# Retention pairs in a two-layer encoder trunk: three block sums per product set written to PSUM and turned or scaled from there, and a new order for the token sums and decay matrices around them

## What is computed

```python
a = rms_norm(h, norm_g[0, 0])
proj = a @ w_in                                  # (1024, 1024) x (1024, 3328)
q, k, v, g, mq = jnp.split(proj, [768, 1536, 2304, 3072], axis=-1)
qh, kh = rotary(q, pos), rotary(k, pos) * 128 ** -0.5
y = forward(qh, kh, vh, decay[0]) + flip(forward(flip(qh), flip(kh), flip(vh), decay[1]))
# forward, in chunks of 128: scores with decay, plus a state that is scanned over chunks
y = silu(g) * group_norm(y)
m = memory_attention(mq, mem_k, mem_v)           # softmax over 256 keys, scale 1/8
h = h + rms_norm(concatenate([y, m]) @ w_out, norm_g[0, 1])
```

## Time and profile before

| | us |
|---|---|
| median of 3 runs | 2235.84 (2235.43 to 2237.63) |
| profiled execution | 2234.97 |
| its span, first to last instruction | 2233.2 |
| TensorE busy | 2192.5 |
| VectorE busy | 1329.0 |
| GpSimd busy | 1199.2 |
| ScalarE busy | 923.5 |
| mean granted TensorE clock | 0.997 of full speed |

### The profile page before, as it was taken

One profiled execution on the slowest core, in us unless ns is written; L12 is line 12 of the kernel. 1 busy time (PEld: TensorE's weight loads), 2 busy tenths in 40 slices (PEclk: granted clock), 3 DMA queues, 4 the chain that ended last, 5 costly groups with the idle time before them and its releaser, 6 DMA issues.

```text
span 2233.2 us, 31950 instructions
## 1 busy us (share of the span) xinstructions
PE 2192.5 (98%) x11542; PEld 1799.5 (81%) x11542; DVE 1329.0 (60%) x2159; ACT 923.5 (41%) x1851; POOL 1199.2 (54%) x953
## 2 busy tenths in 40 slices
PE   9899999999999999999999999999999999999998
PEld 8678777788888888888889877778878888888887
DVE  6867777847644444577773245555575444447767
ACT  6532222456232332344563345465732333234444
POOL 1256666568988888400324243325799888870001
PEclk9999999999999999999999999999999999999999
DMA  8001111543343323563354523344433433338334
GB/s 330 29 29 48 48 48 48 187 181 104 129 146 122 113 95 109 207 230 91 99 189 116 149 68 91 62 140 154 168 108 121 158 99 108 99 118 323 98 96 164
DMA packets 130970, 280.37 MB, mean 126 GB/s; under 512 B 31983, under 2 KB 46590, under 8 KB 128766
## 3 DMA queue, kind: packets, MB, share of 16 engines
q1 hardware_dynamic: 130814, 278.33, 38.4%
HBM read 207.76 MB, written 70.54 MB: 125 GB/s over the span
## 4 chain that ended last, share of the span: by engine, by line
PE 84%; DVE 6%; POOL 3%; issue 2%; ACT 1%; DMA 0%; DVEq 0%; POOLq 0%; ACTq 0%
PE PS L2692 26%; PE PS L2694 25%; PE PS L2693 25%; PE PS L2967 2%; POOL OPS L1101 2%; PE PS L3233 2%; PE PS L3215 1%; PE PS L3133 1%; DVE rtmp L2540 1%; DVE rtmp L2541 1%; PE PS L3000 1%; PE PS L2954 1%; DVE ST L2471 1%; DVE qT L2542 1%; POOL TW L1125 1%
## 5 line engine op out<-in xcount | busy, mean ns | idle before, releaser
L2692 PE MATMUL PS<-AOP,OPS 128*128 128x512 f32 x1216 | 474.3, 390 | 1.1 <-POOL OPS L1101 0.6
L2694 PE MATMUL PS<-AOP,OPS 128*128 128x512 f32 x1216 | 473.2, 389 | 0.0
L2693 PE MATMUL PS<-AOP,OPS 128*128 128x512 f32 x1216 | 473.1, 389 | 0.0
L1101 POOL TENSOR_TENSOR OPS<-TW,OPS 128x512 fp32r<-128x512 f32 x174 | 263.2, 1526 | 78.6 <-ACT OPS L1464 77.4
L1035 POOL TENSOR_TENSOR wlo<-stage,whi 128x512 fp32r<-128x512 f32 (+1 forms) x120 | 153.7, 1304 | 218.5 <-ACT whi L1357 218.3
L2692 PEld LDWEIGHTS PS<-AOP,OPS 128*128 128x128 f32 x1216 | 228.3, 188 | 51.5 <-POOL OPS L1101 2.4
L2694 PEld LDWEIGHTS PS<-AOP,OPS 128*128 128x128 f32 x1216 | 228.3, 188 | 47.4
L2693 PEld LDWEIGHTS PS<-AOP,OPS 128*128 128x128 f32 x1216 | 228.3, 188 | 47.0
L1464 ACT ACTIVATE OPS<-TW 128x512 fp32r<-128x512 f32 x176 | 106.6, 628 | 343.7 <-POOL TW L1125 321.4
L2692 PE MATMUL PS<-OPS 128*128 128x512 f32 x584 | 227.7, 390 | 0.3
L2694 PE MATMUL PS<-OPS 128*128 128x512 f32 x584 | 227.2, 389 | 0.0
(11 more groups left out here) (339 smaller groups left out, 4755.4 us busy)
## 6 DMA issues: line engine op xcount, KB each, us to landing
stage<-in_w SPq DMA_DIRECT2D x100, 512.0 KB, 3.8
hidden_scratch<-HT SPq DMA_DIRECT2D x154, 256.0 KB, 2.2
SRAW<-hidden_scratch SPq DMA_DIRECT2D x154, 256.0 KB, 2.7
stage<-in_wpack SPq DMA_DIRECT2D x76, 512.0 KB, 3.8
BW<-in_w SPq DMA_DIRECT2D x16, 1024.0 KB, 8.4
h_scratch<-Hb SPq DMA_DIRECT2D x24, 512.0 KB, 3.8
Hb<-h_scratch SPq DMA_DIRECT2D x24, 512.0 KB, 5.9
cat_scratch<-OC SPq DMA_DIRECT2D x14, 512.0 KB, 3.0
```

The costliest lines, as they stand in the source:

```text
L1101: pool.tensor_tensor(place[:, 1, :], w1_operand(l, j, p), place[:, 0, :].bitcast(F32), ALU.subtract)\
L2692: pe.matmul(dst, stat[0], mov[0], start=start, stop=False, skip_group_check=onto)
L2693: pe.matmul(dst, stat[0], mov[1], start=False, stop=False, skip_group_check=onto)
L2694: return pe.matmul(dst, stat[1], mov[0], start=False, stop=stop, skip_group_check=onto)
```

## The change

1. The sums "22", "21" and "12" are written to PSUM: "22" into bank 6, "21" and "12" over their own bank. The rotations and scalings read them there; `turn_pairs` works in the bank and its last operation writes SBUF. Its first operation has no wait behind it any more. A bank is free for its next product only when the rotation or scaling is done (`bank_out`), where it was free after the sum.
2. VectorE's order per head: `query_second` directly behind "21", ahead of "12" and `group_norm`; `key_first` behind `value_first`, ahead of "u3".
3. The first token sum (s_one) is made before memory attention; the further sums move to steps 1 to 4, the remainder to 11 to 14. The decay matrices move to steps 10 to 15 (ScalarE) and 11 to 16 (VectorE).
4. At the first head: ScalarE's `block_hi(0)` comes before the gate and `block_hi(1)` behind it, `token_his_late(0)` behind the values; GpSimd's `block_lo(0)` comes first; `first_sum_lo` goes behind "u2"; two of the four `token_lo_late` go from GpSimd to VectorE, ahead of the scan.

```diff
-            for item in (("u2", a), ("u3", a), ("22", a), ("11", a), ("21", a), ("12", a), ("u2", b), ("query", h), ("11", b),
-                         ("u3", b), ("key", h), ("22", b), ("21", b), ("value", h), ("12", b), ("gate", h)):
+            for item in (("u2", a), ("u3", a), ("22", a), ("11", a), ("22 out", a), ("21", a), ("query", h), ("12", a),
+                         ("u2", b), ("11", b), ("key", h), ("u3", b), ("22", b), ("21", b), ("value", h), ("22 out", b),
+                         ("12", b), ("gate", h)):
...
+        def ret_sum_at(r, which):
+
+            if which in ("u2", "u3"):
+                return ret_block(r, "12" if which == "u2" else "22")
+            return ret_bank({"22": "6", "21": "4", "12": "3"}[which])
+
+        def bank_out(p, r):
+
+            even = r % 2 == 0
+            h = 1 + r // 2
+            return summed(*{"1": ("11", r), "6": ("22 out", r), "7": ("query", h) if even else ("value", h),
+                            "5": ("key", h) if even else ("gate", h)}[p])
...
@@ GpSimd
+                if r == 0:
+                    block_lo(0)
                 weight_sum(r, "5")
                 weight_sum(r, "6")
-                block_lo(7 * r)
+                if r:
+                    block_lo(7 * r)
...
                 if h == 1:
-                    for k in range(4):
+                    for k in range(2, 4):
                         token_lo_late(k)
...
@@ ScalarE
-                if 4 <= t < 4 + RH:
-                    h = t - 4
+                if 10 <= t < 10 + RH:
+                    h = t - 10
...
                     if u == 3:
+                        block_hi(0)
                         act.wait_ge(*EV[n])
                         gate(0)
-                        block_hi(0)
-                if t == steps(RUN_A0) - 1:
-                    act.wait_ge(*USED[U_RETH + 3])
-                    token_his_late(0)
+                        block_hi(1)
...
                     if h == 1:
-                        block_hi(1)
+                        token_his_late(0)
                         block_hi(2)
                         token_his_late(1)
...
@@ VectorE, before memory attention
+            for k in range(4):
+                g1, g2 = gT[:, GAIN[1], k:k + 1], gT[:, GAIN[1], 4 + k:5 + k]
+                link(dve.tensor_scalar(xraw[:, 1, 4 + k, :], xraw[:, 1, 4 + k, :], g2, None, ALU.mult))
+                dve.scalar_tensor_tensor(out=xraw[:, 1, 4 + k, :], in0=xraw[:, 1, k, :], scalar=g1,
+                                         in1=xraw[:, 1, 4 + k, :], op0=ALU.mult, op1=ALU.add).then_inc(s_one, 1)
...
-                if 5 <= t < 5 + RH:
+                if 11 <= t < 11 + RH:
...
@@ VectorE, sums and rotations
-                dve.tensor_tensor(ret_block(r, dst), ret_bank(bank), ret_block(r, with_), ALU.add).then_inc(c_sum, 1)
+                dve.tensor_tensor(ret_sum_at(r, what), ret_bank(need), ret_sum_at(r, with_), ALU.add).then_inc(c_sum, 1)
...
-            def turn_pairs(dst, src, cols):
-
-                link(dve.tensor_tensor(rtmp[0:64, :], src[64:128, :], ropeS[64:128, cols], ALU.mult))
-                link(dve.tensor_tensor(rtmp[64:128, :], src[0:64, :], ropeS[0:64, cols], ALU.mult))
-                link(dve.tensor_tensor(dst, src, ropeC[:, cols], ALU.mult))
-                return dve.tensor_tensor(dst, dst, rtmp[:, :], ALU.add)
+            def turn_pairs(dst, bank, cols):
+
+                dve.tensor_tensor(rtmp[0:64, :], bank[64:128, :], ropeS[64:128, cols], ALU.mult)
+                link(dve.tensor_tensor(rtmp[64:128, :], bank[0:64, :], ropeS[0:64, cols], ALU.mult))
+                link(dve.tensor_tensor(bank, bank, ropeC[:, cols], ALU.mult))
+                return dve.tensor_tensor(dst, bank, rtmp[:, :], ALU.add)
...
             def key_first(r):
 
                 dve.wait_ge(*summed("12", r))
-                dve.wait_ge(*summed("query", r // 2 + 1))
-                turn_pairs(ret_block(r, "12"), ret_block(r, "12"), T0).then_inc(c_sum, 1)
+                turn_pairs(ret_block(r, "12"), ret_sum_at(r, "12"), T0).then_inc(c_sum, 1)
...
@@ VectorE, order of a head
                     product_sum(r, "u2")
+                    if h == 1:
+                        first_sum_lo()
                     block_lo(r)
+                    if h == 1:
+                        for k in range(2):
+                            token_lo_late(k)
                     scan(h, lambda c: product_sum(r, "u3") if c == 3 else None)
                     product_sum(r, "22")
                     query_first(r)
                     key_second(r)
                     product_sum(r, "21")
+                    query_second(r)
                     product_sum(r, "12")
                     group_norm(h)
                     product_sum(r + 1, "u2")
-                    query_second(r)
                     block_lo(r + 1)
                     value_first(r + 1)
+                    key_first(r)
                     product_sum(r + 1, "u3")
-                    key_first(r)
                     product_sum(r + 1, "22")
...
@@ TensorE
                 elif r:
-                    pe.wait_ge(*summed({"1": "11", "6": "u2", "7": "21", "5": "12"}[p], r - 1))
+                    pe.wait_ge(*bank_out(p, r - 1))
```

More of the change, by code:

```diff
@@ L279, in trunk_program @@
         s_one, s_diff, s_two, s_hi, s_lo = sem("s_one"), sem("s_diff"), sem("s_two"), sem("s_hi"), sem("s_lo")
-        s_hi_late, s_lo_one, s_lo_four = sem("s_hi_late"), sem("s_lo_one"), sem("s_lo_four")
+        s_hi_late, s_lo_one, s_lo_four, s_lo_pool = (sem(n) for n in ("s_hi_late", "s_lo_one", "s_lo_four", "s_lo_pool"))
         q_sum, q_hi, q_lo, q_lo_dve, q_used = (sem(n) for n in ("q_sum", "q_hi", "q_lo", "q_lo_dve", "q_used"))
@@ L2504, in token_sums @@
                                              in1=xraw[:, 0, k, :], op0=ALU.mult, op1=ALU.add).then_inc(s_two, 1)
-                if 6 <= t < 10:
-                    k = t - 6
+                if 11 <= t < 15:
+                    k = t - 11
                     dve.wait_ge(s_hi, 2 * k + 1)
@@ L2509, in token_sums, with token_lo_late @@
                                              in1=sum_hi[:, 0, k, :].bitcast(F32), op0=ALU.mult, op1=ALU.subtract).then_inc(s_lo_one, 1)
+            def token_lo_late(k):
+                dve.wait_ge(s_hi_late, 5 + k)
+                dve.tensor_tensor(sum_lo[:, 0, 4 + k, :], xraw[:, 0, 4 + k, :], aT[:, 1, 1, k, :].bitcast(F32),
+                                  ALU.subtract).then_inc(s_lo_four, 1)
             def first_sum_lo():
@@ L2518, in product_sum @@
             def product_sum(r, what):
-                need, dst, bank, with_ = {"u2": ("6", "12", "6", "12"), "u3": ("7", "22", "7", "12"), "22": ("5", "22", "5", "22"),
-                                          "21": ("4", "21", "4", "12"), "12": ("3", "12", "3", "12")}[what]
+                need, with_ = {"u2": ("6", "u2"), "u3": ("7", "u2"), "22": ("5", "u3"), "21": ("4", "u2"), "12": ("3", "u2")}[what]
                 if what == "u2":
                     dve.wait_ge(c_one, r + 1)
-                elif what in ("u3", "21", "12"):
-                    dve.wait_ge(*summed("u2", r))
                 else:
-                    dve.wait_ge(*summed("u3", r))
+                    dve.wait_ge(*summed(with_, r))
                 dve.wait_ge(q_used, 7 * r + RET_ORDER.index(need) + 1)
-                dve.tensor_tensor(ret_block(r, dst), ret_bank(bank), ret_block(r, with_), ALU.add).then_inc(c_sum, 1)
+                dve.tensor_tensor(ret_sum_at(r, what), ret_bank(need), ret_sum_at(r, with_), ALU.add).then_inc(c_sum, 1)
             def block_lo(r):
@@ L2573, in value_first, with scaled_block @@
                 dve.tensor_tensor(ret_block(r, "11"), ret_bank("2"), xrow[:, T0], ALU.mult).then_inc(c_sum, 1)
[L2575 to L2580 removed]
+            def scaled_block(r, which):
                 dve.wait_ge(*summed(which, r))
[L2583 to L2584 removed]
+                dve.tensor_tensor(ret_block(r, which), ret_sum_at(r, which), xrow[:, T0 if which == "12" else T1],
+                                  ALU.mult).then_inc(c_sum, 1)
             for t in range(steps(RUN_A0) + 1):
@@ L2599, in _ @@
                             take_gate(0, (ago,))
-            first_sum_lo()
             for h in range(1, RH + 1):
@@ L2814, in first_set_free @@
                 last = 2 * (RH - 1) - 1
-                return lambda i: [summed(("11", "u2", "21", "12")[i], last)] + ([(ktok_rdy, 2 * RH - 1 + i)] if i < 2 else [])
+                return lambda i: [bank_out("1675"[i], last)] + ([(ktok_rdy, 2 * RH - 1 + i)] if i < 2 else [])
             def turn_second(l, part, tiles=range(TT)):
```

37 lines of the change are left out of this document (12 added, 25 removed).

## The result

The changed kernel takes **2214.4 us** (median of 4 runs, 2213.6 to 2216.3) against 2236.1 for the kernel before (2235.4 to 2237.6): ratio **0.9903** [0.9886, 0.9920], 21.7 us less. Forecast were 2212.2 and 23.6 us. Two things that the change does not touch make up about as much as that 1.9: TensorE's start is 0.84 late (its projections begin at 23.25 instead of 22.38; over all the traces from 22.3 to 23.6), and it waits once for 1.2 on GpSimd at 542, in layer 0's dense block, which none of the other traces has.

A forecast was written before the change was run, and what follows sets the result against it. TensorE, busy 2192.5 of 2233.2 us, was taken as the bound, its waits on VectorE's slow rotations the main gain. 10.5 + 2.5 + 2.6 + 8.0 = 23.6 us off 2234.97, plus 0.9 for the median: 2212.2, range 2204 to 2221.

The forecast's parts named there:

- the seven pairs from 142.1 on: First head, VectorE between "u2" and the scan: seven SBUF pairs, four slow and three fast, scan starting at 151.3.
- 1, the rotations: Retention heads: sums in PSUM make VectorE's operations 0.69 us, 2.75 a block, 9.3 us less VectorE work per head.
- 2, the heads: TensorE's waits before "5" and "3" go, 0.1 us a head returns: 10.5 us in heads 2 to 4, 2.5 in head 5.
- 3, the first head: First retention head: nothing net up to its outputs, 2.6 us gained behind them, bounds 0 to 5.
- net up to the outputs: 0: First head before its outputs: waits removed and new waits before "2" and "4" cancel.
- 4, memory attention: Memory attention: moved token sums and decays gain 8.0 us, bounds 1 to 11.9, with a new TensorE stop of 2.9 us.
- (a): Rival: memory attention gains nothing, its stops and low clock only move earlier; about 2219 us, chance 0.17.
- (b): Rival: everything goes, heads, first head and all memory attention stops; 32 us gained, 2204 us, chance 0.12.
- (c): Rival: working in the PSUM bank is dear, 1.65 us per in-place operation, "5" waits longer; 2217 us, chance 0.10.
- (d): Rival: ScalarE's and GpSimd's weight splits come late behind VectorE, half of the 16.2 us stays; 2220 us, chance 0.06.
- (e): Rival: slower, the new stop near 58 lets the clock fall and later memory attention waits keep it low; 2240 us, chance 0.03.
- signs of being wrong: In-place operations above 0.8 us, TensorE idle over 1 us per head, clock below 1 after 80, or losses behind 450.

The follow-up runs named there:

- heads_only: Kernel before with only the heads' part: sums in PSUM, VectorE's new order in the heads, waits on the banks; 2218.0 us, ratio 0.9924.
- diffs_early: Changed kernel with GpSimd's four token differences moved from behind its weight remainders into its earlier idle time; 2211.2 us, ratio 0.9890.
- first_head2: Changed kernel, first head reordered: ScalarE's first_product before the second four token copies, sum "22" before VectorE's one remainder (GpSimd three), "3"'s before query decays; 2209.3 us.
- sbuf_sums: Changed kernel with the sums in SBUF again and banks free at the sums, VectorE's new order kept; 2240.0 us, ratio 1.0019.
- second_late: Changed kernel with VectorE's second token part back at steps 3 to 6 of memory attention; 2217.1 us, ratio 0.9919.
- early_only: Kernel before with only the new token sums, decays and first head's splits, the heads' sums still in SBUF; 2231.9 us, ratio 0.9984.
- psum_old_order: Changed kernel with sums still in PSUM but query_second and key_first back at their old places in VectorE's order; 2247.0 us, ratio 1.0054.
- decays_early: Changed kernel with the decay matrices and token remainders sum_lo back at their old steps; 2216.2 us, ratio 0.9913.
- first_sum_only: Changed kernel with second token part, decays and token remainders at their old steps; in memory attention only the first token sum stays moved; 2218.3 us, ratio 0.9923.

## Why the prediction was right, and where it was off

The mechanism was the forecast one, but that the time came out within 2.2 us is in part luck. By the marks the terms were off by +1.2 (heads), -2.9 (first head), -2.7 (memory attention) and -0.4 (behind the sixth head), 4.9 us in all before rounding: 18.7 instead of 23.6. The other 3.0 came back because one profiled execution lay above its median and the other below. Two slips in the working do not change this: 0.67 + 2.15 - 0.3 is 2.5, not 2.6, and the seven pairs from 142.1 on end at 150.8, not 151.3.

**1, the rotations: right.** Forecast: 0.69 us an operation in the bank, 2.75 us a block. Measured: the in-place operation L2559 700 ns, the others 684 to 693, 2.87 us a block (VectorE by form):
```profile
L2559 DVE TENSOR_TENSOR PS<-PS,ropeC 128x512 f32<-128x512 f32 x20 | 14.0, 700 | 0.7
L2557 DVE TENSOR_TENSOR rtmp<-PS,ropeS 64x512 f32<-64x512 f32 x20 | 13.9, 693 | 0.7
```
Writing PSUM costs nothing measurable. I took the lower bound by inference from reading, which no row on writing backed; it held. Only the pitch of 0.60 for two operations with no wait between was wrong; it is 0.71 here (262.06, 262.77).

**2, the heads: right, slightly low.** Forecast 10.5 for heads 2 to 4, 2.5 for head 5 and 2.6 for the first head behind its outputs, 15.6; the marks give 0.5 + 14.8 + 1.4 = 16.8, `heads_only` 17.0. A head wins 3.7 us where I had 3.49. The new wait on the bank of `key_first` is 0.15 to 0.16 us where I had 0.1.

**3, the first head: the mechanism right, the size wrong.** The step that failed is "net up to the outputs: 0"; it was -2.9. Timelines of VectorE, GpSimd and TensorE, the last row from `diffs_early`:
```profile
136.75 4.75 DVE L2535 TENSOR_TENSOR sum_lo<-xraw,aT 128x512 fp32r<-128x512 f32 x4
141.42 1.76 DVE L2553 TENSOR_TENSOR wop_a<-wsum_a,wop_a 128x512 fp32r<-128x512 f32 x1
143.10 4.59 DVE L2528 TENSOR_TENSOR sum_lo<-xraw,aT 128x512 fp32r<-128x512 f32 x2
144.81 2.89 DVE L2528 TENSOR_TENSOR sum_lo<-xraw,aT 128x512 fp32r<-128x512 f32 x1
150.17 0.69 DVE L2546 TENSOR_TENSOR kT<-PS,kT 128x512 f32<-128x512 f32 x1
...
144.30 5.61 POOL L1281 TENSOR_TENSOR qfb<-qT,QD 128x1024 f32<-128x1024 f32 x2
...
136.25 0.47 PE L2706 MATMUL PS<-aT,wop_a 128*128 128x512 f32 x1 [2.23 <-ACT kT L1790]
...
151.01 0.47 PE L2706 MATMUL PS<-aT,wop_b 128*128 128x512 f32 x1 [3.23 <-DVE kT L2546]
...
147.37 0.47 PE L2709 MATMUL PS<-aT,wop_b 128*128 128x512 f32 x1 [3.23 <-DVE kT L2549]
```
The wait of 2 us before "2" is there as forecast. The seven pairs of VectorE took 4.75 + 1.76 + 4.59 = 11.1 us, where four at 1.65 and three at 0.70 us are 8.7: most of them had GpSimd beside them, which worked without a gap beside the last three. The last one (144.81, a part of the row above it) took 2.89 us, more than the 1.66 that I had as the upper bound: beside it stood GpSimd's product of 128x1024, 2.8 us for each. The stop before "4" is 3.2 instead of 2.0 us. And behind it the clock falls, which I had not counted: granted 0.57 in 152 to 156, eight matmuls at a pitch of 0.43 instead of 0.23 us. `first_head2` shows the cause by removing it.

How much this clock costs is a matter of the execution. Eight traces have this same first head up to its outputs. In three (the changed kernel, `sbuf_sums`, `second_late`) the clock falls behind the stop before "4", and the outputs come 31.6 us behind the scores. In three (`early_only`, `psum_old_order`, `decays_early`) it falls earlier, behind the stop before "2"; the time lost there comes off the next stop, which is VectorE's and shrinks from 3.2 to 1.6 us. In two (`diffs_early`, `first_sum_only`) it does not fall at all. In these five the outputs come 29.9 to 30.0 us behind the scores. So the stops alone cost 1.3 us against the kernel before, and the low clock 1.6 more in the execution that was profiled.

**4, memory attention: right in kind; 8.0 forecast, 5.3 measured by the marks, 6.1 without the late start.** The first token sum was free, as forecast (of VectorE's wait of 5.10 us before memrow 0.33 is left). The step that failed is the start of the scores of step 4, 60.6; they came at 62.64, those of step 8 at 81.30 instead of 78.2; 0.84 of each is the late start. Timelines of GpSimd, VectorE and TensorE, and a window:
```profile
51.62 6.00 POOL L1218 TENSOR_TENSOR xraw<-xraw 128x512 f32<-128x512 f32 x4
52.44 2.33 DVE L2289 TENSOR_SCALAR SB<-SB,rowinv 128x256 f32<-128x256 f32 x2
54.70 1.77 DVE L2515 SCALAR_TENSOR_TENSOR xraw<-xraw,gT 128x512 f32<-128x512 f32 x1
56.51 1.66 DVE L2517 SCALAR_TENSOR_TENSOR xraw<-xraw,gT 128x512 f32<-128x512 f32 x1
58.09 1.21 DVE L2255 TENSOR_REDUCE maxraw<-PS 128x4 f32<-128x1024 f32 x1
...
61.45 0.63 PE L2981 MATMUL PS<-ident,SB 128*128 128x128 f32 x4 [3.15 <-ACT PT L1683]
62.64 1.28 PE L2968 MATMUL PS<-bdK_ret,MQ 64*128 64x256 f32 x8 [0.57 <-ACT SB L1662]
...
81.30 1.13 PE L2968 MATMUL PS<-bdK_ret,MQ 64*128 64x256 f32 x8 [0.64 <-ACT SB L1662]
...
64.00:68.00 4.00, 4.00 (x12) 3.18 (x13) 3.78 (x10) 3.40 (x13) 0.00 (x0) 0.64 0.01 4
```
The two token sums of step 1 start at 54.70 where I had 52.3. Of these 2.4 us 0.84 is the late start and the rest is the scaling of step 0, which I had priced at its own speed and which took 2.33 us beside GpSimd instead of 0.62. So the peaks of step 2 are complete at 59.6, not 57.1, and all that follows keeps the distance of 2 to 3 us. The clock fell to 0.64 in 64 to 68 and was at full speed from there to the first head.

**Rivals.** (a) falls with 5.3 us gained in memory attention; (b) with both new stops; (c) with L2559 at 700 ns: the page "VectorE: DVE Perf Modes" of the Trainium skill (Rules for kernel authors) would have the sums in SBUF, and `sbuf_sums` shows what that costs here, 25.9 us; (d) with the heads' gain, no split was late; (e) with the clock at full speed from 68 on to the end of memory attention. But its mechanism, a clock that falls behind stops, is 10.1 of the 12 us by which `psum_old_order` is slower than the kernel before. Of the signs of being wrong two came up, both small: the clock was below 1 after 80, at 0.57 in 152 to 156, and 0.4 us were lost behind the heads, where the stop of 1.2 at 542 stands.

## What to carry to other kernels

Before calling VectorE the bound, look whether its operations are at their own speed: two SBUF inputs beside a busy GpSimd cost 1.65 us instead of 0.69, and leaving one input in PSUM wins it all back. What the company cost went by GpSimd's operation: about 1 us beside 128x512, for VectorE's small scaling (0.31 to 1.2) as for its pair (0.69 to 1.65), and 2.2 beside 128x1024. A bank that keeps a sum must be emptied in the order in which TensorE comes for it again; operations of 0.7 us in the wrong order gave a longer kernel than those of 1.65. And price every moved operation by what GpSimd does at its new time, and every stop of about 3 us with up to 2.4 us more for the low clock that can follow it, unless the next stop is another engine's and takes the loss up.

## What the runs showed of the hardware that was not expected

- GpSimd's company slows more than pairs: VectorE's scaling of a 128x256 block from SBUF to SBUF, with one tensor input, took 1.2 us beside GpSimd (2.33 for two at 52.44) and 0.31 alone (0.62 for two).
- An operation that reads and writes the same bank takes 0.70 us on 128x512, as from SBUF to SBUF alone (0.69).
- A VectorE operation on 128x512 with two SBUF inputs took 0.69 us alone, 1.65 to 1.78 beside GpSimd's 128x512 operations and 2.89 beside its 128x1024 product (144.81 in the changed kernel).
- Behind a stop of 3 us in the heads the clock was down from the first matmul on in four heads of `psum_old_order`, down only after 1.2 us in its other head (restart at 235.21) and in the changed kernel (restart at 151.01), and not at all in `diffs_early` and `first_sum_only`, whose stop before the same product is as long (3.23 us up to 147.37 and up to 154.10; granted clock 1.00 in 145 to 155 and in 152 to 160). Which of these happens was not settled.
